# Three return buffers, a later difference and weight sums built pair by pair beside the gates, in a two-layer streaming-encoder trunk

## The reference

```python
for i in range(DEPTH):                       # DEPTH = 2
    h = rms_norm(x, g_mix_pre[i])
    z = h @ w_in[i]                          # aq, ak, av, af, bcq, bckv, bkpe, cq, ck, cv
    ya, yb, yc = fox(z), mla(z), window(z)   # each 512 x 512
    gates = jax.nn.sigmoid(h @ w_gate[i] + b_gate[i])
    ga, gb, gc = jnp.split(gates, 3, axis=-1)
    merged = ga * (ya @ w_branch_a[i]) + gb * (yb @ w_branch_b[i]) + gc * (yc @ w_branch_c[i])
    x = x + rms_norm(merged @ w_out[i], g_mix_post[i])
    u = causal_dwconv(rms_norm(x, g_ffn_pre[i]) @ w_up[i], conv_w[i], conv_b[i])
    f = (jax.nn.gelu(u[..., :2816]) * u[..., 2816:]) @ w_down[i]      # w_down[i]: 2816 x 1024
    x = x + rms_norm(f, g_ffn_post[i])
    x = x + rms_norm(sigmoid(rms_norm(x, g_ple_pre[i]) @ w_ple_gate[i]) * (p[i] @ w_ple[i]), g_ple_post[i])
```

## Time and profile before

| | us |
|---|---|
| median of 3 runs (2014.5 to 2018.82) | 2018.8 |
| the profiled execution, its own time | 2018.37 |
| its span | 2016.5 |
| PE busy | 1856.6 (92%) |
| DVE busy | 1157.0 (57%) |
| ACT busy | 934.8 (46%) |
| POOL busy | 288.9 (14%) |

### The profile page before, as it was taken

The page is one execution under the profiler, slowest core; times in us unless marked ns, Lnnn a source line. Parts: engine busy times, 40 slices in busy tenths (PEclk is TensorE's granted clock), DMA queues, the critical chain, the costliest instruction groups (busy, mean ns, idle before and its releaser), DMA issues.

```text
span 2016.5 us, 26796 instructions
## 1 busy us (share of the span) xinstructions
PE 1856.6 (92%) x9111; PEld 1525.5 (76%) x9111; DVE 1157.0 (57%) x1784; ACT 934.8 (46%) x1660; POOL 288.9 (14%) x274
## 2 busy tenths in 40 slices
PE   9649999999999999788996599999999999998888
PEld 8538888878888888666884388887888888876667
DVE  4425655555477777456544256555455777774575
ACT  4426645643354444334544276456434444443453
POOL 1000200111023333101010001001111133331010
PEclk9779999999999999998998699999999999999989
DMA  7993244224414333565379922442243233435652
GB/s 235 268 177 100 74 114 99 87 74 146 136 54 126 109 109 117 179 212 193 93 253 242 178 70 85 109 104 74 84 146 115 82 110 110 125 120 179 216 170 84
DMA packets 312680, 270.20 MB, mean 134 GB/s; under 512 B 64100, under 2 KB 264448, under 8 KB 312320
## 3 DMA queue, kind: packets, MB, share of 16 engines
q1 hardware_dynamic: 297992, 222.50, 37.1%
q0 software_dynamic: 14208, 46.14, 9.3%
q10 hardware_dynamic: 376, 0.21, 0.1%
HBM read 253.54 MB, written 59.24 MB: 155 GB/s over the span
## 4 chain that ended last, share of the span: by engine, by line
PE 53%; DVE 13%; DMA 10%; issue 8%; SPq 8%; ACT 7%; ACTq 1%; DVEq 1%; POOL 0%; POOLq 0%
PE psum L881 43%; DMA q_raw<-qspill 5%; SPq L716 5%; DMA raw<-in_w_in_dram 3%; ACT wh L1505 2%; PE psum L1196 2%; SPq L814 2%; DVE cg L2410 2%; PE psum L1177 2%; DVE cg L2412 2%; PE psum L1162 2%; DVE wl L1959 2%; ACT cg L1733 2%; DVE ft_both L2412 2%; DVE ft_both L2410 2%
## 5 line engine op out<-in xcount | busy, mean ns | idle before, releaser
L881 PE MATMUL psum<-xnh,wh 128*128 128x512 f32 (+1 forms) x1424 | 574.4, 403 | 89.7 <-issue 89.7
L1959 DVE TENSOR_TENSOR wl<-raw,wh 128x1024 fp32r<-128x1024 f32 (+2 forms) x276 | 374.6, 1359 | 331.8 <-ACT wh L1505 331.5
L881 PE MATMUL psum<-xnh,wl 128*128 128x512 f32 (+1 forms) x1424 | 555.1, 390 | 0.0
L881 PE MATMUL psum<-xnl,wh 128*128 128x512 f32 (+1 forms) x1424 | 554.7, 390 | 0.0
L1505 ACT ACTIVATE wh<-raw 128x1024 fp32r<-128x1024 f32 (+2 forms) x276 | 282.5, 1025 | 328.2 <-PE psum L881 176.7
L881 PEld LDWEIGHTS psum<-xnh,wh 128*128 128x128 f32 x1424 | 273.3, 192 | 150.2 <-issue 100.2
L881 PEld LDWEIGHTS psum<-xnh,wl 128*128 128x128 f32 x1424 | 271.3, 191 | 56.4
L881 PEld LDWEIGHTS psum<-xnl,wh 128*128 128x128 f32 x1424 | 272.6, 191 | 47.1
L2185 DVE CUSTOM_DVE_ANT_0 Sp<-psum,ptok 128x128 f32<-128x128 f32 (+3 forms) x128 | 62.8, 491 | 118.6 <-issue 63.8
L2688 POOL TENSOR_TENSOR merged<-merged,th 128x512 f32<-128x512 f32 x32 | 41.2, 1288 | 323.8 <-DVE th L2317 323.8
L1737 ACT ACTIVATE cg<-cg 128x512 f32<-128x512 f32 x44 | 27.8, 633 | 128.7 <-DVE cg L2412 128.7
(11 more groups left out here) (332 smaller groups left out, 3485.5 us busy)
## 6 DMA issues: line engine op xcount, KB each, us to landing
raw<-in_w_up_dram SPq DMA_DIRECT2D x88, 512.0 KB, 3.7
raw<-in_w_gate_dram SPq DMA_DIRECT2D x48, 512.0 KB, 3.7
row_sums<-in_w_down_dram POOLq DMA_DIRECT2D x4, 5632.0 KB, 29.2
col_sums<-in_w_down_dram POOLq DMA_DIRECT2D x4, 5632.0 KB, 55.4
raw<-in_w_down_dram SPq DMA_DIRECT2D x44, 512.0 KB, 4.6
raw<-in_w_in_dram SPq DMA_DIRECT2D x30, 512.0 KB, 4.7
raw<-row_sums SPq DMA_DIRECT2D x22, 512.0 KB, 3.7
raw<-col_sums SPq DMA_DIRECT2D x22, 512.0 KB, 4.5
```

The costliest lines, as they stand in the source:

```text
L881: ins = pe.matmul(out, left, right, start=start and n == 0, stop=stop and n == 2)
L1959: dve.tensor_tensor(low[:, 0:n], raw[(L * NCH + c) % RAW][:, 0:n], hi[:, 0:n].bitcast(F32), ALU.subtract).then_inc(w_lo.sem, 1)
```

## The change

It does three things.

1. **Weight sums.** `weight_sums(L)` no longer issues four large DMAs (5.5 MB each) at the start of the layer. It is called twelve times, `weight_sums(L, s)` after POOL's additions 0 to 11 of `merged`. Call s waits for the copies of pair s - 1, issues two accumulating DMAs for pair s - 1 and two plain copies for pair s, 512 KB each.
2. **Feature sums.** `q_raw` has three buffers in place of two, with a semaphore each. SP issues the load of pair j right after the load of chunk n = `Q_PREP[j]`, before three chunks later; the first seven `Q_PREP` are 8, 10, ... 20 in place of 6, 8, ... 18.
3. **Difference.** DVE's `diff` of a pair stands after the low part of that pair's `dn_cols` chunk, not before it; `fours_taken` moves from n = 25 to n = 26 and 28.

```diff
-Q_PREP = [2 * j + 6 for j in range(7)] + [26, 28, 30, 32]
+Q_PREP = [2 * j + 8 for j in range(7)] + [26, 28, 30, 32]
-    q_back = Tally(sem("q_back"), 16 * PAIRS)
+    q_back = [Tally(sem(f"q_back{i}"), 16 * len(range(i, PAIRS, 3))) for i in range(3)]
-    q_raw = [here(f"q_raw{i}", 96 + 3 * i, [P, 768]) for i in range(2)]
+    q_raw = [here(f"q_raw{i}", 96 + 3 * i, [P, 768]) for i in range(3)]
...
-                wait(wsum_in.sem, wsum_in.at(L, 32))
+                wait(wsum_in.sem, wsum_in.at(L, 32 * PAIRS))
...
-                    if c == ST_DOWN + Q_PREP[j] + 3:
+                    if c == ST_DOWN + Q_PREP[j]:
...
-                        if j >= 2:
-                            wait(q_lo.sem, q_lo.at(L, j - 1))
-                        sp.dma_start(q_raw[j % 2][:, :], qspill[L, :, j, :]).then_inc(q_back.sem, 16)
+                        if j >= 3:
+                            wait(q_lo.sem, q_lo.at(L, j - 2))
+                        sp.dma_start(q_raw[j % 3][:, :], qspill[L, :, j, :]).then_inc(q_back[j % 3].sem, 16)
...
             for n in range(3, 4 * PAIRS):
                 q = n - 2 * PAIRS
-                if q >= 0 and q % 2 == 0:
+                if q >= 0 and q % 2 == 1:
                     diff(L, q // 2)
                 if n == 2 * PAIRS + 2:
                     threes_taken(L, 0)
                     threes_taken(L, 1)
                 lo(L, ST_DOWN + n)
-                if n == 2 * PAIRS + 3:
+                if n == 2 * PAIRS + 4:
                     fours_taken(L, 0)
+                if n == 2 * PAIRS + 6:
                     fours_taken(L, 1)
...
-            pool.dma_start(row_sums[L], rows[L, 0]).then_inc(wsum_copied.sem, 16)
-            pool.dma_start(col_sums[L], cols[L, 0]).then_inc(wsum_copied.sem, 16)
-            pool.wait_ge(wsum_copied.sem, wsum_copied.at(L, 32))
-            pool.dma_start(row_sums[L], rows[L, 1], accum_op=ALU.add).then_inc(wsum_in.sem, 16)
-            pool.dma_start(col_sums[L], cols[L, 1], accum_op=ALU.add).then_inc(wsum_in.sem, 16)
+            def pair(j):
+                return slice(2 * j, 2 * j + 2)
+
+            if s > 0:
+                pool.wait_ge(wsum_copied.sem, wsum_copied.at(L, 32 * s))
+                pool.dma_start(col_sums[L, :, pair(s - 1), :], cols[L, 1, :, pair(s - 1), :], max_dma_last_dim=2048,
+                               accum_op=ALU.add).then_inc(wsum_in.sem, 16)
+                pool.dma_start(row_sums[L, :, s - 1:s, :], rows[L, 1, :, s - 1:s], max_dma_last_dim=4096,
+                               accum_op=ALU.add).then_inc(wsum_in.sem, 16)
+            if s < PAIRS:
+                pool.dma_start(col_sums[L, :, pair(s), :], cols[L, 0, :, pair(s), :]).then_inc(wsum_copied.sem, 16)
+                pool.dma_start(row_sums[L, :, s:s + 1, :], rows[L, 0, :, s:s + 1]).then_inc(wsum_copied.sem, 16)
...
-            weight_sums(L)
             window_queries_lo(L)
...
                                        ).then_inc(m_added.sem, 1)
+                    s = KT * (br - 1) + m
+                    if s <= PAIRS:
+                        weight_sums(L, s)
```

More of the change, by code:

```diff
@@ L361, in trunk_kernel @@
     q_spilled = Tally(sem("q_spilled"), 16 * PAIRS, 16)
-    q_back = Tally(sem("q_back"), 16 * PAIRS)
+    q_back = [Tally(sem(f"q_back{i}"), 16 * len(range(i, PAIRS, 3))) for i in range(3)]
     q_hi = Tally(sem("q_hi"), PAIRS)
     q_lo = Tally(sem("q_lo"), PAIRS)
-    wsum_copied = Tally(sem("wsum_copied"), 32)
-    wsum_in = Tally(sem("wsum_in"), 32)
+    wsum_copied = Tally(sem("wsum_copied"), 32 * PAIRS)
+    wsum_in = Tally(sem("wsum_in"), 32 * PAIRS)
     diff_made = Tally(sem("diff_made"), PAIRS)
@@ L1750, in sums_hi @@
         def sums_hi(L, j):
-            act.wait_ge(q_back.sem, q_back.at(L, 16 * (j + 1)))
+            act.wait_ge(q_back[j % 3].sem, q_back[j % 3].at(L, 16 * (j // 3 + 1)))
             act.wait_ge(w_used.sem, w_used.at(L, ST_DOWN + 2 * j + 2))
-            act.activation(qh[:, j, :], q_raw[j % 2][:, :], ACT.Copy).then_inc(q_hi.sem, 1)
+            act.activation(qh[:, j, :], q_raw[j % 3][:, :], ACT.Copy).then_inc(q_hi.sem, 1)
         def products_out(L):
@@ L2041, in sums_lo @@
             dve.wait_ge(q_hi.sem, q_hi.at(L, j + 1))
-            dve.tensor_tensor(ql[:, j, :], q_raw[j % 2][:, :], qh[:, j, :].bitcast(F32), ALU.subtract
+            dve.tensor_tensor(ql[:, j, :], q_raw[j % 3][:, :], qh[:, j, :].bitcast(F32), ALU.subtract
                               ).then_inc(q_lo.sem, 1)
@@ L2609, in window_queries_lo, with weight_sums @@
                                        ).then_inc(qc_lo.sem, 1)
-        def weight_sums(L):
+        def weight_sums(L, s):
             rows = A["w_down"].rearrange("l (j m p) c -> l m p j c", m=2, p=P)
             cols = A["w_down"].rearrange("l (t p) (h c) -> l h p t c", p=P, h=2)
-            pool.dma_start(row_sums[L], rows[L, 0]).then_inc(wsum_copied.sem, 16)
-            pool.dma_start(col_sums[L], cols[L, 0]).then_inc(wsum_copied.sem, 16)
-            pool.wait_ge(wsum_copied.sem, wsum_copied.at(L, 32))
-            pool.dma_start(row_sums[L], rows[L, 1], accum_op=ALU.add).then_inc(wsum_in.sem, 16)
-            pool.dma_start(col_sums[L], cols[L, 1], accum_op=ALU.add).then_inc(wsum_in.sem, 16)
+            def pair(j):
[9 more added lines that the diff above has]
+                pool.dma_start(row_sums[L, :, s:s + 1, :], rows[L, 0, :, s:s + 1]).then_inc(wsum_copied.sem, 16)
         def features_apart(L, it):
```

## The result

| | us |
|---|---|
| before, median of 4 runs (2013.08 to 2018.82) | 2016.65 |
| changed kernel, median of 4 runs (1899.96 to 1905.81) | 1903.88 |
| ratio | 0.944 [0.9416, 0.9463] |
| the profiled execution, its own time | 1905.19 |

What follows compares the result with a forecast made beforehand. PE was busy 92% of the span, so gains had to come from its idle time at each layer's front and in the down projection. 2018.4 - 108 + 30 - 2 x 14.8 - 2 x 10 = 1891 us, range 1852 to 1932.

Steps and rivals of the forecast that it cites:

- 1a front: Start of each layer: without the weight sums' transfers there, attention begins sooner; 108 us gained (bounds 90 and 116).
- 1b gates: Gates stage: the moved weight-sum transfers make additions 9 and 11 late; 15 us lost per layer, 30 us together.
- 2 stage 1: Down projection, first stage: feature sums return sooner and ACT's wait disappears; 14.8 us gained per layer.
- 3 stage 2: Down projection, second stage: sooner returns and the later difference bring it to 56 us; 10 us gained per layer.
- P: Gates: period of one weight-sum step on POOL, from transfers, an issue and a landing's fixed part; taken as 12.5 us.
- The walk: Gates: step-by-step timing of POOL's steps and additions; two late additions cost 8.2 and 8.6 us, 17 us per layer.
- Nothing in mixer 1: Gates: mixer 1's steps come in pairs 25 us apart or more and catch up, so no PE idling there.
- The serial line: Down projection, stage 2: high part, low part, difference, high part take near 3.9 us a pair, about 4.7 for four pairs.
- A (no stall): Gates: steps turn in 9.5 us or less, or issues are much shorter, so additions come in time; 1861 us, chance 0.18.
- B (starved loads): Gates: POOL's packets crowd out chunk loads and PE runs at the loads' pace; 1925 us, chance 0.16.
- C (half of the gain in down): Down projection: loads and returns together become the bound, 12 of 24.8 us gained per layer; 1917 us, chance 0.09.
- E (the front not freed): Layer front: another wait already stood behind the weight sums, so half its gain; 1945 us, chance 0.04.

Runs made afterwards that it cites:

- clear rows: Changed kernel with no weight-sum step behind additions 4 and 5, and steps 4 to 11 behind additions 6 to 13: 1922.92 us, ratio 0.9514.
- the kernel with six early steps: Changed kernel with weight-sum steps 0 to 5 before the latents, the others in twos behind additions 1, 3 and 5: 1901.96 us, ratio 0.943.
- the spread one: Changed kernel with the twelve steps spread over mixer A's attention, window queries, latents and mixer 1, none in mixer 2: 1874.3 us, ratio 0.9281.
- the last kernel: The spread one with the difference before the low part, steps 5 and 6 waiting for all but one of gates A's chunks: 1849.45 us, ratio 0.9163.
- copies-first: Changed kernel with each step's plain copies issued ahead of its accumulating DMAs: 1891.99 us, ratio 0.9384.
- lagged: Changed kernel with step s accumulating pair s - 2, not s - 1, and two semaphores for the copies: 1890.24 us, ratio 0.937.

## Why the prediction was nearly right, and where it missed

| term | forecast | measured in both layers |
|---|---|---|
| 1a front | -108 | -117.2 |
| 1b gates | +30 | +50.6 |
| 2 stage 1 | -29.6 | -31.3 |
| 3 stage 2 | -20 | -15.5 |
| sum | -127.6 | -113.4 |

**Part 1a** held. The attention began at 94.68 where 95.8 was forecast, with PE busy throughout at full clock; the two attentions give 57.9 + 54.7 = 112.6 us. Another 4.7 us came until the first additions, in whose stretch the attention had started at the lower clock before (0.48 us a matmul in place of 0.22). The forecast called this "a little more" and gave it no number.

**Part 1b is the term that was mis-sized**: 15 us per layer, measured 25.9 and 24.7. Its mechanism and its period were right. P was taken as 12.5 and is 12.7. `mh` waited twice, as said. The Trainium skill's figure for such DMAs ("DMA: Bandwidth & Descriptors", section "Anatomy of one DMA — SWDGE (gpsimd) path") made it 12.8, if the four ran one after another; the period in this trace agrees. The picture behind it does not: it gives one DMA 3.2 us, and here they took 8.7 and 9.5 us to land (medians), with the four issues beginning within 2.1 us.

Three things were off, in layer 0:

- The walk gave 8.2 and 8.6 us for the two late additions, and the sum cut these 16.8 to 15 because P would shrink. P did not shrink. The second cost 8.6 us as walked (lag 14.6 to 23.2), and in clear rows, where nothing is late ahead of them, the first two make a lag of 9.3 and 17.7 us. PE's own stops are only 5.98 + 6.77 = 12.8 us of it, since slow matmuls from the pause before fill a part of each wait.
- "Nothing in mixer 1" was wrong, and this is the larger step. The last row sums of the attention beside it returned in 10.45 us, PE stood 5.60 us, and step 6 and all later ones began 5.9 us late. The walk had followed only what is queued behind POOL's waits, not who else has a short DMA on the same engines. The kernel with six early steps and the spread one stop at the same kind of round trip, and clear rows, whose row sums came back in 2.9 us, does not stop there.
- The clock behind each pause was not priced: 6.8 us in all from 380 to 470. Behind the last pause it adds 2.8 us to the lag; there no later wait takes it in.

PE's own account is 12.8 + 5.6 + 6.8 = 25.2 us. The account by steps is 16.8 + 5.9 + 2.8 = 25.5. The loss is 25.9.

**Parts 2 and 3.** Stage 1 took 53.4 and 53.3 us (n = 2 stands at 783.95 in layer 0), down 15.9 and 15.3, against 14.8 forecast. Waits for `q_raw` fell from 115.4 to 0.2 us. Stage 2 was to take 56 us and took 58.0 and 57.8. The serial line was underestimated in its first pairs. The chain in the changed kernel's stage 2, second pair:

```profile
845.97 1.05 ACT wh L1505
847.04 1.23 DVE wl L1959
848.27 0.60 DVE ydn L2060
848.87 0.60 DVE ydn L2061
849.47 0.86 DVE ql L2042
850.33 0.61 DVE raw L2036
851.57 1.05 ACT dn_wh L1505
```

From high part to high part it is 5.6 us for this pair and the first, where 3.9 to 4.7 were forecast: beside `ql` (0.86), which the forecast had, the removal of results (1.2) stands ahead of the difference, and ACT waits for it. The third takes 7.6, with ACT's squares of the results in it, and the next two 3.8 and 4.4. Putting the difference behind the low part earns nothing here: the old place was 3.0 and 0.5 us faster in stage 2, with returns equally soon. `q_raw`'s third buffer is worth nothing either.

That the sum came within 13 us is in part luck: 9 us that the front gave above its term stand against 21 that the gates took.

**The rivals.** A (no stall) didn't happen where the steps stood, but the last kernel shows that its end is reachable by placing them. B (starved loads) wasn't the limit of the change; it is the next one, into which the copies-first and lagged kernels ran. C (half of the gain in down) and E (the front not freed) fell: 46.9 of 49.6 and all of the front came.

## What to carry to other kernels

Background DMA traffic has no price of its own; its price is that of what it makes late. List the short DMAs whose latency is bare (round trips through DRAM at the end of a phase) and the engine work queued behind the issuing engine's waits, and place the traffic away from both: here that turned 49 us into nothing at the same bytes. Where a wait throttles such traffic, removing the wait uncovers the starved loads next, so move the traffic first. To each pause of TensorE add the slower work behind it, here over a third of the pause again (6.8 on 18.4 us).

## What was unexpected of the hardware

- A DMA share near or above 0.96 did not say that loads were late. From 230 to 260 us in the last kernel the share is 1.09 and 0.96 with PE busy all the time; at 0.99 in mixer 2 of the lagged kernel a chunk load took 26.5 us. What differs was not taken apart.
- Beside a step everything on the DMA engines is slower, not the small transfers alone. Of what is issued from 375 to 385 us, the 128 KB returns land in 9.9 us in the change and in 2.9 in clear rows, the 512 KB gate chunk in 10.8 and 4.0. The chunk's delay is hidden by four buffers, the return's by nothing.
- POOL's additions to `merged` right behind four DMA issues show 1.98 to 2.07 us in the trace where they take 1.3 otherwise, behind two issues too (1.33 and 1.35). The trace's times on POOL are rough, and no run tests a cause.
